# A gap of 192 bytes between the weight ring and the activation tiles of a transformer kernel

## The reference

```
h = LN(ALPHA*h + 0.5*swiglu(h, w_gate, w_up, w_down))          # twice, around the two stages below
h = LN(ALPHA*h + concat(hgrn2(h @ w_in), gating(h @ w_in)) @ w_out)
h = LN(ALPHA*h + attention(h @ wq, mem @ wk, mem @ wv) @ wo)
z = modulate(h, c) @ w_in_2                                    # 1024 x 8704
ya, yb, yc = neighbourhood_attention(z, ctx), short_conv(z), conformer(z)
out = h + gate * ((ga*(ya @ oa) + gb*(yb @ ob) + gc*(yc @ oc)) @ w_o)
```

## Time and profile before

| | |
|---|---|
| runs | 1709.17, 1709.23, 1710.14 us |
| profiled execution, span from the first to the last instruction | 1706.6 us |
| granted TensorE clock, mean | 1.000 |
| DMA over the span | 188 MB, mean 110 GB/s |

### The profile page before, as it was taken

How to read it: one execution, slowest core, us unless ns; L and a number is a source line. 1 busy time by engine, 2 the same in 40 slices (tenths; PEclk the granted TensorE clock), 3 DMA queues, 4 the chain that set the end, 5 groups by cost and what they waited for, 6 DMA issues and landing times.

```text
span 1706.6 us, 22901 instructions
## 1 busy us (share of the span) xinstructions
PE 1691.5 (99%) x8500; PEld 1394.7 (82%) x8500; DVE 994.7 (58%) x1341; ACT 683.6 (40%) x975; POOL 166.8 (10%) x158
## 2 busy tenths in 40 slices
PE   9999999999999999999999999999999999999999
PEld 7888888888787888888888888877778787788887
DVE  5333339987965784666333333457976869844442
ACT  4222232246454465434222223346454445732330
POOL 0000000112004521013000000013011020000000
DMA  5333247633122353223332233323333222243331
GB/s 216 98 98 98 91 138 231 222 121 119 52 98 66 109 182 137 67 82 123 98 98 94 92 130 117 109 87 118 85 99 95 86 83 86 74 123 109 104 109 62
DMA packets 51476, 188.05 MB, mean 110 GB/s; under 512 B 5776, under 2 KB 6288, under 8 KB 50512
## 3 DMA queue, kind: packets, MB, share of 16 engines
q1 hardware_dynamic: 44640, 161.50, 29.7%
q10 hardware_dynamic: 5184, 16.00, 2.9%
q0 software_dynamic: 1584, 9.60, 1.6%
HBM read 182.89 MB, written 4.19 MB: 110 GB/s over the span
## 4 chain that ended last, share of the span: by engine, by line
PE 89%; DVE 7%; ACT 2%; issue 1%; DMA 0%; POOL 0%; SPq 0%; DVEq 0%; ACTq 0%; POOLq 0%
PE proj L422 83%; DVE w_lo L414 1%; PE aux L1859 1%; PE aux L1846 1%; PE aux L1619 1%; PE aux L1836 1%; DVE y L2016 0%; ACT w_hi L407 0%; DVE score L1221 0%; DVE qk L1264 0%; DVE md L1242 0%; PE aux L566 0%; DVE qk L1265 0%; PE aux L1839 0%; DVE md L1241 0%
## 5 line engine op out<-in xcount | busy, mean ns | idle before, releaser
L414 DVE TENSOR_TENSOR w_lo<-raw,w_hi 128x1024 fp32r<-128x1024 f32 x300 | 380.5, 1270 | 388.8 <-ACT w_hi L407 382.0
L422 PE MATMUL proj<-a_hi,w_hi 128*128 128x512 f32 (+1 forms) x1536 | 600.8, 391 | 3.3 <-DVE a_lo L909 1.8
L422 PE MATMUL proj<-a_hi,w_lo 128*128 128x512 f32 (+1 forms) x1536 | 591.3, 385 | 0.0
L422 PE MATMUL proj<-a_lo,w_hi 128*128 128x512 f32 (+1 forms) x1536 | 591.0, 385 | 0.0
L407 ACT ACTIVATE w_hi<-raw 128x1024 fp32r<-128x1024 f32 x300 | 315.3, 1053 | 233.4 <-PE proj L422 164.3
L422 PEld LDWEIGHTS proj<-a_hi,w_hi 128*128 128x128 f32 x1536 | 288.5, 188 | 67.9 <-issue 5.8
L422 PEld LDWEIGHTS proj<-a_lo,w_hi 128*128 128x128 f32 x1536 | 288.7, 188 | 58.4 <-issue 2.9
L422 PEld LDWEIGHTS proj<-a_hi,w_lo 128*128 128x128 f32 x1536 | 288.5, 188 | 58.5
L422 PE MATMUL proj<-hid_hi,w_hi 128*128 128x512 f32 (+1 forms) x374 | 142.6, 381 | 0.0
L422 PE MATMUL proj<-hid_hi,w_lo 128*128 128x512 f32 (+1 forms) x374 | 140.9, 377 | 0.0
L422 PE MATMUL proj<-hid_lo,w_hi 128*128 128x512 f32 (+1 forms) x374 | 140.8, 377 | 0.0
(11 more groups left out here) (368 smaller groups left out, 2011.1 us busy)
## 6 DMA issues: line engine op xcount, KB each, us to landing
raw<-stream SPq DMA_DIRECT2D x303, 512.0 KB, 3.5
ctxk<-ada_in ACTq DMA_DIRECT2D x12, 512.0 KB, 3.7
ctxv<-ada_in ACTq DMA_DIRECT2D x12, 512.0 KB, 3.9
out<-h ACTq DMA_DIRECT2D x7, 256.0 KB, 2.0
h<-x_in SPq DMA_DIRECT2D x3, 512.0 KB, 8.7
btab<-rpb_in POOLq DMA_DIRECT2D x4, 384.0 KB, 3.5
cond_row<-cond_in ACTq DMA_DIRECT2D x1, 1024.0 KB, 5.9
side<-mem_in POOLq DMA_DIRECT2D x1, 1024.0 KB, 5.2
```

Source lines behind the costliest of these rows:

```text
L414: nc.vector.tensor_tensor(w_lo[:, st.slot], raw[:, st.slot], w_hi[:, st.slot].bitcast(F32), ALU.subtract).then_inc(lo_ready, 1)
L422: mm = nc.tensor.matmul(dst, a, b, start=start and n == 0, stop=stop and n == 2)
```

## The change

Two tiles are declared that nothing reads or writes. The first, of 48 values (192 bytes), stands behind `w_lo` and ahead of `h`; it lasts for the whole kernel, so every tile that is declared later begins 192 bytes further on. The second, of 80 values (320 bytes), stands behind `xs` and ahead of `ctx_hi`, in the scope of the memory and the context; `ctx_hi` and `ctx_lo` thus begin 512 bytes further on than before. Each engine's instructions and waits, and their order, are the same as before.

```diff
--- before.py
+++ after.py
@@ -172,6 +172,7 @@
         raw = sb("raw", [P, RING, SB * P])
         w_hi = sb("w_hi", [P, RING, SB * P], F32R)
         w_lo = sb("w_lo", [P, RING, SB * P], F32R)
+        sb("gap_behind_weights", [P, 48])
         h = sb("h", [P, KD, T])
         with ExitStack() as ph:
             cond_row = sb("cond_row", [P, 2, D], F32, ph)
@@ -237,6 +238,7 @@
             xp = sb("xp", [P, 2, 2, M], F32, ph)
             xpt_hi, xpt_lo = (sb(n, [P, 2, MB, M], F32R, ph) for n in ("xpt_hi", "xpt_lo"))
             xs = sb("xs", [P, 3, 8, 2], F32, ph)
+            sb("gap_ctx", [P, 80], F32, ph)
             ctx_hi = sb("ctx_hi", [P, KD, M], F32R, ph)
             ctx_lo = sb("ctx_lo", [P, KD, M], F32R, ph)
         with ExitStack() as ph:
```

## The result

The changed kernel takes 1743.86 us (median of four runs, 1743.1 to 1744.41), the kernel before 1709.2 on the same occasion: a ratio of 1.0203 with a 95% interval of 1.0188 to 1.0217. It is 34.7 us slower, where the prediction had 42 us faster.

A forecast was written before the change was run, and what follows sets the result against it. TensorE's matmul stream was taken as the bound. Gains 40.6 + 3.8 + 2.3 = 46.7 us, x 0.92 = 43.0, less 1 is 42: span 1664.6, plus 2.6 is 1667.2 us; range 1652 to 1688.

The forecast's parts named there:

- What bounds the kernel: TensorE's matmuls in product(), 83% of the span; the distance between two starts, 226.7 ns at 512 columns, sets the time.
- the relative place of moving tile and weights sets the surcharge: Ring products: time beside the columns, 13.3 ns at equal places modulo 512 bytes, 6.7 ns with the moving tile 192 off.
- the rival of no effect: Whole kernel: the offset does nothing and ctx is faster for an unseen reason; 1709 us, chance 0.07.
- The price at 256 columns: Products moving 256 columns: 6.7 ns saved per matmul, 120.0 to 113.3 ns, 3.8 us for 564 matmuls.
- I carry it over to 512: Products moving 512 columns: the same 6.7 ns saved per matmul as at 256, for an expected distance of 220.0 ns.
- The term of 6054 matmuls: Forward products with a moving activation of 512 columns: 6054 x 6.7 ns, a gain of 40.6 us.
- The token-major products: 336 products with 512 columns of weights moving and the activation loaded: a gain of 2.3 us, bounds +4.5 to -4.5.
- ctx unchanged: Context keys, 96 matmuls at 256 columns: offset stays at 192 bytes, distance stays at 113.3 ns.
- The share on the path: Whole kernel: 92% of the saved matmul time shortens the run, 46.7 us becoming 43.0.
- The norms' waits: TensorE's waits at the norms are below 1 us each; 1 us taken off the gain for chains coming out.
- The 2.6 us between span and time: Median of runs 1709.2 against profiled span 1706.6; this 2.6 us was added to the forecast span.
- The rival that came true: 512-column forward matmuls in product(): the offset brings two reads together, 6.7 ns more each; 1746 us, chance 0.04.

The follow-up runs named there:

- run 2: Kernel before plus 192 bytes ahead of the weight ring, so weights and activations move together: 1708.22 us, ratio 0.9999.
- run 3: Kernel before plus a gap of 256 bytes behind w_lo and none ahead of the context: 1708.32 us, ratio 1.0001.
- run 4: Kernel before plus a gap of 64 bytes behind w_lo: 1721.38 us, ratio 1.0073.
- run 5: Kernel before plus 192 bytes behind w_lo and 64 behind ctxv, so h and a stand at 192, the stages' tiles at 256: 1734.72 us, ratio 1.0156.
- run 6: Kernel before plus 192 bytes behind ctxv and 320 ahead of ctx_hi, nothing behind w_lo, so only the stages' tiles stand at 192: 1717.39 us, ratio 1.0052.
- run 1: Kernel cut to its products alone, moving tile offset 0 to 1024 bytes; at 192 bytes 233.3 ns at 512 columns, 113.3 at 256; no whole-kernel time.
- run 7: Kernel cut to its products alone, four offsets, 512 to 192 moving and 128 to 32 loaded columns; distances between matmul starts measured, no whole-kernel time.
- run 9: Kernel before with only side_hi and side_lo moved 192 bytes on, and 64 bytes added behind them: 1709.4 us, ratio 1.0006.

## Why the prediction was wrong

- *What bounds the kernel* was right: the time followed the distance of two matmuls, in the changed kernel and in runs 2 to 6.
- *That the relative place of moving tile and weights sets the surcharge* was right (runs 1, 2, 5, 6), as against the rival of no effect. That the reads of load and matmul meet is the prediction's picture of it, which no run shows. Its period is 256 bytes, and not the 512 that the prediction reckoned with; for an offset of 192 this makes no difference.
- *The price at 256 columns* was right: 6.7 ns forecast, 113.3 ns measured for a, side, hid and m once a stretch has settled, 6.0 ns less than before with the starts of the stretches in it.
- *The step that failed* is "I carry it over to 512, because at equal places the surcharge is the same at both widths". It is the same there, 32 cycles, and is so at offset 0 only. At 192 it is 16 cycles at 256 columns and 48 at 512 (run 1), and run 7 has other values between. The term of 6054 matmuls, put at -40.6 us, measured +6.7 ns each, +40.4 us. In the kernel before no moving tile of 512 columns stood off the weights' place, so the trace could not show this.
- *The token-major products*, put at -2.3 us, with bounds of 4.5 either way, lost 2.2 ns each, +0.7 us.
- *ctx unchanged* was wrong: its distance rose from 113.3 to 117.7 ns with the same offset, and stayed there for all its 96 matmuls. In runs 2, 5 and 6, with the same offset again, it was 113.4 to 113.6. In run 6 ctx and the weights stand at the very addresses of the changed kernel. So the same work can go on in more than one rhythm, as the memory's keys of run 6 show too. What decides which wasn't tried. It is 0.4 us here.
- *The share on the path* was right: with the measured prices the sum is 40.4 - 564 x 6.0 / 1000 + 0.7 + 0.4 = 38.1 us, and 92% of it 35.1, against 34.7 measured.
- *The norms' waits* were misread: the prediction has them below 1 us each, but the one in the memory's keys was 1.6 us already. There a faster matmul only makes a longer wait, and the half clock behind it costs about 1 us, as much as was won (run 9).
- *The 2.6 us between span and time* came from two different executions. Where the record has both for one, they are 1.6 apart (1744.41 and 1742.8 in the changed kernel). It doesn't bear on the sign.
- *The rival that came true* had 1746 us and a chance of 0.04. Its sign and its place were those measured (longer distances at 512 columns, in product(), the 6054 forward matmuls); that the offset "brings the two reads together" is not shown. Its price of 6.7 ns was measured as well, but by luck: it was the figure of 256 columns with its sign turned. The argument held against it, that the widths behave alike at equal places, was one point of a curve. The chance was too low for a case of which the trace had no example.

The Trainium skill says in "TensorE: Matmul & The Clock Gate", section "Step-by-step: what each phase is for", that the weight load and the moving operand have read ports of their own and that a load takes no read bandwidth from the running matmul. If that were all, the place of one tile against the other could not matter. These runs disagree for float32r: between two offsets that differ in nothing else, a matmul of 512 columns takes 226.7 or 233.3 ns. Whether it is the reads of the load that cost this is not shown.

What is open: how the offset, the width and the number of loaded columns give these values. The runs show the surcharge, not the reads that meet.

## What to carry to other kernels

Where one matmul with its own weight load follows another and TensorE is the bound, the bytes between the loaded and the moving tile, modulo 256, are worth up to 3% of a matmul's distance at 512 columns and up to 6% at 256, in float32r; no other type was tried. Here at 512 columns the offset was best at 0, at 256 columns at 192; a gap must be tried at the width that carries the time, and a price from another width isn't one. A small kernel of products alone gave the whole curve in one run and forecast four whole kernels to within 2 us (runs 3 to 6). And where TensorE waits for another engine soon after, as at the norm in the memory's keys, a faster matmul brought nothing.

## What the runs showed that I had not expected

- The best offset turns over with the width: 0 against 192 bytes is 32 against 48 cycles at 512 columns, and 32 against 16 at 256.
- The period is 256 bytes, half of what a weight block takes per partition.
- Loading fewer columns at offset 0 doesn't lower the surcharge at 512 moving columns (34 cycles with 128 loaded, 44 with 32), though it does at 256 (32 and 16).
- One offset and one width can settle in two rhythms: the context's keys at 113.3 or at 117.7 ns in two kernels, the memory's keys of run 6 at both in one.
- The longer wait at the norm was followed by 3.4 us at half clock, which cost as much as 192 faster matmuls had won (run 9).
